# Split partition sums: two 256-column products of a high and a low part for seven of nine float32 products

## The reference

```python
def rms_norm(x, g):
    y = x * lax.rsqrt(jnp.mean(x * x, axis=-1, keepdims=True) + 1e-6)
    return y * g

for i in range(2):
    x = x + 0.5 * swiglu(rms_norm(x, ffn1_norm[i]), ffn1_w_in[i], ffn1_w_out[i])
    x = x + mixer_i(rms_norm(x, mix_norm[i]))
    x = x + 0.5 * swiglu(rms_norm(x, ffn2_norm[i]), ffn2_w_in[i], ffn2_w_out[i])

# in the retention, per head (512 features), before the gate and the output projection
out = out * lax.rsqrt(jnp.mean(out * out, axis=-1, keepdims=True) + 1e-6)
```

## Time and profile before

| what | value |
|---|---|
| median of three runs | 1019.72 us |
| the profiled execution: its time, its span | 1019.98 us, 1017.9 us |
| TensorE products busy | 1013.1 us (100% of the span) |
| VectorE busy | 779.9 us (77%) |
| ScalarE busy | 496.9 us (49%) |
| GpSimd busy | 98.4 us (10%) |
| chain that ended last | TensorE 92%, VectorE 4%, ScalarE 2% |

### The profile page before, as it was taken

The page is one execution under the profiler, slowest core; times in us unless marked ns, Lnnn a source line. Parts: engine busy times, 40 slices in busy tenths (PEclk is TensorE's granted clock), DMA queues, the critical chain, the costliest instruction groups (busy, mean ns, idle before and its releaser), DMA issues.

```text
span 1017.9 us, 15878 instructions
## 1 busy us (share of the span) xinstructions
PE 1013.1 (100%) x5922; PEld 885.5 (87%) x5922; DVE 779.9 (77%) x874; ACT 496.9 (49%) x536; POOL 98.4 (10%) x91
## 2 busy tenths in 40 slices
PE   9999999999999999999999999999999999999998
PEld 8888888888888888888888888888887898888888
DVE  7988867788788687787767787788668977877743
ACT  7455445544444364454444454464447944554432
POOL 0000013100100161000013100000320041000000
PEclk9999999999999999999999999999999999999999
DMA  9664455653543454554455645534553244544461
GB/s 349 239 244 169 142 187 208 247 208 114 201 181 124 166 196 152 201 195 175 152 179 198 246 165 203 192 143 149 197 228 128 105 158 194 207 165 167 154 191 65
DMA packets 32293, 185.29 MB, mean 182 GB/s; under 512 B 3840, under 2 KB 6400, under 8 KB 16128
## 3 DMA queue, kind: packets, MB, share of 16 engines
q1 hardware_dynamic: 31968, 184.64, 49.2%
q10 hardware_dynamic: 288, 0.16, 0.1%
HBM read 183.73 MB, written 1.05 MB: 182 GB/s over the span
## 4 chain that ended last, share of the span: by engine, by line
PE 92%; DVE 4%; ACT 2%; SPq 1%; DMA 1%; issue 1%; POOL 0%; ACTq 0%; POOLq 0%; DVEq 0%
PE ps L1148 92%; DVE w_lo L645 1%; ACT w_hi L333 1%; DMA stage<-w_in_dram 1%; ACT s_two L523 0%; DVE sm L981 0%; SPq L289 0%; SPq L287 0%; PE ps L1448 0%; DVE hs L872 0%; DVE q_a L818 0%; ACT x_sq L618 0%; DVE q_a L812 0%; DVE q_b L815 0%; POOL y_sq L1134 0%
## 5 line engine op out<-in xcount | busy, mean ns | idle before, releaser
L1148 PE MATMUL ps<-h,w_hi 128*128 128x512 f32 x1664 | 581.0, 395 | 0.1
L1148 PE MATMUL ps<-h,w_lo 128*128 128x256 f32 x1664 | 462.2, 278 | 0.0
L645 DVE TENSOR_TENSOR w_lo<-stage,w_hi 128x2048 fp32r<-128x2048 f32 (+1 forms) x190 | 397.0, 2098 | 26.8 <-ACT w_hi L333 26.5
L1148 PEld LDWEIGHTS ps<-h,w_hi 128*128 128x128 f32 x1664 | 311.8, 187 | 71.9 <-DVE w_lo L645 0.4
L333 ACT ACTIVATE w_hi<-stage 128x2048 fp32r<-128x2048 f32 (+1 forms) x190 | 326.8, 1728 | 6.7 <-PE ps L1148 6.2
L1148 PEld LDWEIGHTS ps<-h,w_lo 128*128 128x128 f32 x1664 | 312.8, 188 | 0.5
L1148 PE MATMUL ps<-act_t,w_hi 128*128 128x512 f32 (+1 forms) x726 | 245.8, 388 | 0.0
L1148 PE MATMUL ps<-act_t,w_lo 128*128 128x256 f32 x704 | 196.3, 279 | 0.0
L1148 PEld LDWEIGHTS ps<-act_t,w_hi 128*128 128x128 f32 x726 | 134.7, 188 | 29.9
L365 ACT ACTIVATE tmp<-ps 128x1024 f32<-128x1024 f32 x44 | 45.1, 1026 | 194.1 <-PE ps L1148 194.1
L1148 PEld LDWEIGHTS ps<-act_t,w_lo 128*128 128x128 f32 x704 | 132.6, 188 | 0.0
(11 more groups left out here) (158 smaller groups left out, 739.0 us busy)
## 6 DMA issues: line engine op xcount, KB each, us to landing
stage<-w_in_dram SPq DMA_DIRECT2D x85, 1024.0 KB, 4.8
stage<-w_out_dram SPq DMA_DIRECT2D x64, 704.0 KB, 4.1
stage<-w_ret_dram SPq DMA_DIRECT2D x24, 1024.0 KB, 4.9
stage<-w_ret_out_dram SPq DMA_DIRECT2D x8, 1024.0 KB, 4.8
stage<-w_q_dram SPq DMA_DIRECT2D x4, 1024.0 KB, 4.8
stage<-w_o_dram SPq DMA_DIRECT2D x4, 1024.0 KB, 4.8
stage<-w_in_dram SPq DMA_DIRECT2D x8, 256.0 KB, 3.9
stage<-w_in_dram SPq DMA_DIRECT2D x2, 512.0 KB, 6.1
```

The lines of the kernel that those rows point to most:

```text
L645: nc.vector.tensor_tensor(w_lo[:, s, 0:n], stage[:, s, 0:n], w_hi[:, s, 0:n].bitcast(F32), ALU.subtract).then_inc(lo_ready, 1)
L1148: return nc.tensor.matmul(out_, w, x_, start=start, stop=stop)
```

## The change

`sum_halves(n)`, new on GpSimd, makes two tiles from `sq_sum`: `sq_hi`, its high part (a multiplication with ones, written in the shorter format), and, after a wait for it, `sq_lo`, the rest (a subtraction). It runs behind each of the seven sums. `sum_pair(n)`, new on TensorE, waits for `sq_lo` and multiplies the ones with `sq_hi` and then with `sq_lo`, adding both in PSUM. Norms 0 and 5 keep the plain product, and the products with two columns stay.

Two places in TensorE's order move. In `ret_head`, `head_sum(c)` goes from between `pair(u)` and `pair(u + 1)` into `pair(u + 1)`, behind its first four blocks. In `retention`, the sum of head 3 goes from behind the early blocks of d = 0 to behind those of d = 1.

```diff
+PAIR_SUM = {RET: 1, 2: HEADS_R + 2, 3: HEADS_R + 3}
...
+    sq_hi = at("sq_hi", [P, T], F32R, misc + 27264)
+    sq_lo = at("sq_lo", [P, T], F32R, aux + 14848)
...
+                if m in PAIR_SUM:
+                    pool.wait_ge(sum_added, added_for(m))
+                    sum_halves(PAIR_SUM[m])
+
+            def sum_halves(n):
+
+                nc.gpsimd.tensor_tensor(sq_hi[:].rearrange("p (a n) -> p a n", a=2),
+                                        sq_sum[:].rearrange("p (a n) -> p a n", a=2), same(ones[:], 2),
+                                        ALU.mult).then_inc(sum_hi, 1)
+                pool.wait_ge(sum_hi, n)
+                nc.gpsimd.tensor_tensor(sq_lo[:], sq_sum[:], sq_hi[:].bitcast(F32), ALU.subtract).then_inc(sum_lo, 1)
...
                 nc.gpsimd.tensor_tensor(sq_sum[:], ysf[:, 0:T], ysf[:, T:2 * T], ALU.add).then_inc(sum_added, 1)
+                pool.wait_ge(sum_added, added_for(RET) + 1 + i)
+                sum_halves(2 + i)
...
+            def sum_pair(n):
+
+                pe.wait_ge(sum_lo, n)
+                matmul(ps[:, SUM, 0:T], ones[:].bitcast(F32R), sq_hi[:], True, False)
+                return matmul(ps[:, SUM, 0:T], ones[:].bitcast(F32R), sq_lo[:], False, True)
...
-                if m != ATT:
-                    last = matmul(ps[:, FIRST_SUM if m in LATE_NORMS else SUM, 0:T], ones[:], sq_sum[:], True, True)
+                if m in PAIR_SUM:
+                    last = sum_pair(PAIR_SUM[m])
+                elif m != ATT:
+                    last = matmul(ps[:, FIRST_SUM, 0:T], ones[:], sq_sum[:], True, True)
...
-            def pair(u, banks, i):
+            def pair(u, banks, i, c=None):
...
                     for o in range(2):
                         last = weight_block(banks + o, u % SLOTS, 2 * k + o, h[:, k, :], k == 0, k == DT - 1)
+                    if c is not None and k == 1:
+                        head_sum(c)
...
                 pair(u, 0, i)
-                head_sum(c)
-                pair(u + 1, 2, i)
+                pair(u + 1, 2, i, c)
...
-                pe.wait_ge(sum_added, added_for(RET) + c)
                 pe.wait_ge(sum_read, sums_before(RET) + c)
-                matmul(ps[:, SUM, 0:T], ones[:], sq_sum[:], True, True).then_inc(sum_done, 1)
+                sum_pair(PAIR_SUM[RET] + c).then_inc(sum_done, 1)
...
                         weight_block(d, (u0 + d) % SLOTS, k, y_t[:, k, :], k == 0, False)
-                    if d == 0:
+                    if d == 1:
                         head_sum(HEADS_R)
```

## The result

The changed kernel takes 1028.35 us, the median of six runs that lie in two groups: 1026.08, 1026.72 and 1026.74, and 1029.96, 1030.0 and 1030.66. The kernel before takes 1019.9 us in six runs. The ratio is 1.0082 with an interval of 1.0073 to 1.0092. Slower was right; the size was not: 2.7 us were forecast, 8.4 came, and the median lies above the top of the range. The profiled execution is one of the upper group, 1030.0 us with a span of 1027.9, so the two profiles differ by 10.0 us.

What follows compares the result with a forecast made beforehand. TensorE, busy throughout at full clock, bounds the kernel by columns streamed and its few standstills. -1.14 (six products) + 3.61 (head 3) + 0.2 (norms 1 and 2) = +2.67 us, so 1022.4 us; range 1021.4 to 1025.0.

Steps and rivals of the forecast that it cites:

- The products: At seven sums on TensorE, a pair takes 0.24 us against 0.43 for the plain product: 0.19 us gained each.
- the stall of 0.24: TensorE's standstill from 344.56 to 344.80, before the sum of head 3, waiting for GpSimd's addition; forecast to be gone.
- The wait for head 3, moved: Later sum delays head 3's norm; TensorE idles 4.06 us before its first block with head 3, 3.61 us later.
- GpSimd's steps: New steps meet VectorE's splits at norms 1 and 2: 0 to 0.3 us each, 0.2 us in all; elsewhere no wait.
- The rival in which GpSimd must wait for both splits: Norm 1: sq_lo comes only at 198.7, TensorE stands still for 2.1 us; 1024.3 us, chance 0.08.
- The clock: TensorE's clock falls in the new idle stretch, slowing blocks behind the wait: 2.26 us more, 1024.7 us, chance 0.17.
- The fifth rival: Smaller loss: the 88 blocks behind the wait run 0.01 us faster each, 0.9 us back; 1021.5 us, chance 0.08.

Runs made afterwards that it cites:

- pairs_ffn: The kernel before with the split products at norms 2 and 3 only, all retention sums plain and in their old places; 1025.13 us, ratio 1.004.
- more_early: The changed kernel with twelve early blocks of d = 3 instead of four; 1028.72 us, ratio 1.0077.

## Why the prediction was wrong in size

**The products.** Right as far as they reach. The pair takes 0.23 us between blocks of the retention, against 0.24 forecast. From the start of the blocks to the one behind the sum of head 3 the difference is -0.75 - 0.37 = -1.12 us. By the prediction's terms it is four products before (norm 1 and heads 0 to 2) and the fifth at 0.19 each and the stall of 0.24, together -1.19 us.

**The wait for head 3, moved.** Right. Forecast: TensorE at its wait at 354.49, first block with head 3 at 358.66, 3.61 us later than before. Measured: the last early product starts at 354.29 and the next would have at 354.41; the first block with head 3 starts at 358.37, 3.32 us later than before. The two numbers aren't of the same thing: the four cheaper products ahead are in another term of the sum, and the whole execution began 0.37 us later, so 3.61 - 0.76 + 0.37 = 3.22 us were to be expected here. VectorE's chain from its first step to its last was 9.36 us before and is 358.32 - 348.95 = 9.37 us now. One reading in it was wrong and did no harm: the row of the plain product that starts at 344.80 is 0.70 us long, so it ended at 345.50 and not at 345.34, and VectorE began 0.04 us behind it, as it does behind the pair now. The forecast had 0.44 us from the start of the pair to VectorE's first step, and 0.43 were measured.

**GpSimd's steps.** The durations were right where the prediction worked them out; at norm 3, where it expected none, the subtraction met a split too (2.68 us), at no cost. In norm 1 the subtraction, begun at 194.22, met the split and took 2.68 us, so sq_lo was there at 196.90, the upper end of the forecast, and TensorE's pair started at 197.05. In norm 2 it came at 396.37 + 2.67 = 399.04. The profile reports no wait of TensorE at either. At norm 2 GpSimd's last addition ends 4.63 us later than before and TensorE comes 4.96 us later, and nothing was lost there. In `pairs_ffn`, where nothing comes late, TensorE waited 0.48 us at norm 2 in two of three profiles; in `more_early` it waited 2.13 us. That this place was called tight but priced at 0.3 us at most is the weak point: the price held only for the times of the kernel before. The rival in which GpSimd must wait for both splits didn't occur.

**The clock.** This rival had a chance of 0.17 and came true, in every profile with the idle stretch of about 4 us. Its price, 2.26 us from the warm-up products, was of the right size: 1.65 us in the profiled execution, 1.2 to 2.6 us in the others. That it came so near is partly luck, since the time was borrowed from another stretch. The Trainium skill, TensorE: Matmul & The Clock Gate, section "Why this matters for your kernels", warns that such a gap brings the half rate back; the granted clock of 0.50 behind 3.81 us of idle time agrees. Behind 1.70 us it stayed at 1.00. What argued against it, that the stretch is short beside the busy time around it, was no evidence: the clock had been full for some 350 us and that didn't help. With this rival the forecast is 1024.7, which lies within the stated range; the rest, 3.7 us, is the next point.

**The step that was missing.** This is the step that failed. The prediction priced the plain product by the time that it takes itself, 0.43 us, and had no term for what it does to the products behind it. In every profile it puts the stream of blocks into the fast pace or keeps it there, with one exception, where a pair stands right ahead of it. The pair leaves the slow pace in 53 of the 60 cases in these profiles; six of the seven others are at norm 1. In the profiled execution this cost 3.32 us between norms 2 and 3 and 1.90 us up to 704 us, four times what all seven cheaper products together save. The trace had it: the prediction used 0.346 us for a block everywhere, but the blocks at 370 us took 0.353 at full clock with no wait. A count of products in equal windows would have shown that the kernel has two paces, and asking where one turns into the other would have led to the sums. The fifth rival even had a pace that changes by 0.01 us for each block, with the other sign and without a cause.

Sum of the terms, profile to profile: +0.37 (start) - 1.12 (products and stall) + 4.07 (idle stretch) + 1.65 (clock) + 3.32 + 1.90 (pace) = +10.19, and -0.17 behind it. The two cheaper products of norms 2 and 3 are within the terms of the pace.

**What stays open.** Why there are two paces, and why a plain product of 256 columns, but no narrow one, leads to the fast one, isn't shown; neither is what decides at norm 1 and norm 2 between two executions of the same program, nor why the pace changes at 355 us in some executions and not in others. Why the half clock has two lengths isn't either, nor why it followed a wait of 2.13 us at norm 2 but not one of 1.70 us at head 3; between these no run was made.

## What to carry to other kernels

Where one engine streams without a gap, count its instructions in equal windows before and after each thing out of turn: a product can be worth more by the rhythm it leaves behind than by its own time. Moving a short product later moves the whole chain that hangs on it; find the slack at the far end of the chain first, and if the engine would stand still for some microseconds, add the price of its clock. A step that is called tight must be priced again for every other arrival time, since mending one wait can send the engine into the next one sooner.

## What the runs showed of the hardware

- At full clock with no wait, a block of a 512-column and a 256-column short product (128x128 weights) takes 0.3467 or 0.3533 us, 1.9% apart, and the pace lasts for hundreds of blocks. Behind a plain product of 256 columns it was fast at every place but one (norm 2 with a pair right ahead of it); behind pairs of 256-column short products in heads 0 to 3 it was slow in every trace, at norm 1 in three of nine; behind the transposes of the keys it was slow too.
- The granted clock fell to 0.50 after 3.8 to 3.9 us of idle time in all eight profiles that have it, and stayed at 1.00 after 1.70 us in one. After 2.13 us at norm 2 it fell, in one.
- A subtraction of GpSimd on 128x256 takes 0.74 us alone and 2.67 us when it meets a split of VectorE with two inputs in SBUF.
